# FFN passages reordered, tile shapes of the first mixer grouped, last square added ahead of the first filter combination

## The reference

```python
for i in range(DEPTH):                      # DEPTH = 2, both token groups
    m = adaln(c, w_mod[i], b_mod[i])        # shift, scale, gate, twice
    h = modulate(x, m[0], m[1])             # rms_norm(x) * (1 + scale) + shift
    x = x + m[2] * mixer_i(h)               # 0: GLA || GQA, 1: Hyena || MLA
    x = x + m[5] * swiglu(modulate(x, m[3], m[4]), w_ffn_in[i], w_ffn_out[i])
y = rms_norm(x) * g_final
```

## Time and profile before

| | us |
|---|---|
| median of 3 runs | 1628.18 (1627.47 to 1628.45) |
| the profiled execution | 1625.22 |
| its span, first to last instruction | 1622.6 |
| PE busy | 1581.8 |
| DVE busy | 1080.9 |
| ACT busy | 736.9 |

### The profile page before, as it was taken

How to read it: one execution, slowest core, us unless ns; L and a number is a source line. 1 busy time by engine, 2 the same in 40 slices (tenths; PEclk the granted TensorE clock), 3 DMA queues, 4 the chain that set the end, 5 groups by cost and what they waited for, 6 DMA issues and landing times.

```text
span 1622.6 us, 27752 instructions
## 1 busy us (share of the span) xinstructions
PE 1581.8 (97%) x11361; PEld 1462.3 (90%) x11361; DVE 1080.9 (67%) x1874; ACT 736.9 (45%) x1308; POOL 35.5 (2%) x41
## 2 busy tenths in 40 slices
PE   6999999999999999999999999999999999999997
PEld 3588897799989999999999996789999999999997
DVE  5634662768857857856874466855888487587486
ACT  5445363646624524423545434344565154254254
POOL 0000000001000000000002002000100000000000
PEclk9999999999999999999999999999999999999999
DMA  9565422035455544545235112002523223232222
GB/s 320 191 219 193 156 80 95 24 94 120 118 148 158 152 119 139 149 137 156 72 95 165 55 43 87 26 1 74 114 79 95 62 79 104 60 97 82 76 66 91
DMA packets 239335, 178.20 MB, mean 110 GB/s; under 512 B 9429, under 2 KB 232843, under 8 KB 238572
## 3 DMA queue, kind: packets, MB, share of 16 engines
q1 hardware_dynamic: 236276, 171.19, 35.0%
q0 software_dynamic: 2016, 4.59, 2.1%
q10 hardware_dynamic: 920, 0.69, 0.2%
HBM read 163.37 MB, written 8.49 MB: 106 GB/s over the span
## 4 chain that ended last, share of the span: by engine, by line
PE 90%; DVE 3%; ACT 3%; SPq 2%; DMA 1%; issue 1%; ACTq 0%; DVEq 0%
PE ua L1123 7%; PE ub L1123 7%; PE ua L1125 7%; PE ua L1124 7%; PE ub L1125 6%; PE ub L1124 6%; PE ua L1587 6%; PE ua L1589 5%; PE ua L1588 5%; PE ub L1587 5%; PE ub L1589 5%; PE ub L1588 5%; PE pm L1037 2%; PE ua L1432 2%; PE pt L1459 1%; SPq L722 1%
## 5 line engine op out<-in xcount | busy, mean ns | idle before, releaser
L2183 ACT ACTIVATE whi<-weight_sums 128x1024 fp32r<-128x1024 f32 x88 | 93.1, 1058 | 71.7 <-DVE weight_sums L2878 47.1
L1587 PE MATMUL ua<-x_mixed_high,whi 128*128 128x322 f32 x352 | 110.6, 314 | 1.9 <-ACT snap L2257 1.8
L1587 PE MATMUL ub<-x_mixed_high,whi 128*128 128x322 f32 x352 | 111.0, 315 | 0.9 <-ACT snap L2257 0.9
L1589 PE MATMUL ua<-x_mixed_high,wlo 128*128 128x322 f32 x352 | 109.2, 310 | 0.0
L1589 PE MATMUL ub<-x_mixed_high,wlo 128*128 128x322 f32 x352 | 109.2, 310 | 0.0
L1588 PE MATMUL ub<-x_mixed_rest,whi 128*128 128x322 f32 x352 | 109.0, 310 | 0.0
L1588 PE MATMUL ua<-x_mixed_rest,whi 128*128 128x322 f32 x352 | 109.0, 310 | 0.0
L2851 DVE TENSOR_TENSOR wlo<-weight_sums,whi 128x1024 fp32r<-128x1024 f32 x88 | 107.2, 1218 | 1.5 <-ACT whi L2183 1.4
L1123 PE MATMUL ub<-hidden_high,whi 128*128 128x384 f32 (+1 forms) x324 | 101.7, 314 | 4.5 <-DVE x L2946 3.5
L1123 PE MATMUL ua<-hidden_high,whi 128*128 128x384 f32 (+1 forms) x324 | 101.0, 312 | 1.6 <-DVE x L2946 1.6
L1125 PE MATMUL ub<-hidden_high,wlo 128*128 128x384 f32 (+1 forms) x324 | 100.1, 309 | 0.0
(11 more groups left out here) (688 smaller groups left out, 4959.8 us busy)
## 6 DMA issues: line engine op xcount, KB each, us to landing
raw<-in_w_ffn_in SPq DMA_DIRECT2D x88, 512.0 KB, 6.0
mod_late<-in_w_mod SPq DMA_DIRECT2D x24, 1024.0 KB, 5.3
raw<-in_w_ffn_out SPq DMA_DIRECT2D x48, 384.0 KB, 4.4
modw<-in_w_mod SPq DMA_DIRECT2D x17, 1024.0 KB, 5.4
raw<-in_w_in_even SPq DMA_DIRECT2D x10, 1024.0 KB, 7.8
raw<-in_w_in_odd SPq DMA_DIRECT2D x7, 1024.0 KB, 5.6
mod_first<-in_w_mod SPq DMA_DIRECT2D x5, 1024.0 KB, 12.3
ssq<-sq POOLq DMA_DIRECT2D x14, 320.0 KB, 4.7
```

Of the source, the lines that this page charges most:

```text
L1587: pe.matmul(dst, wh[:, c], xh, start=first, stop=False, skip_group_check=True)
L1589: ins = pe.matmul(dst, wl[:, c], xh, start=False, stop=last, skip_group_check=True)
L2183: act.activation(ring(whi, g, w), src, ACT.Copy).then_inc(g_hi, 1)
```

## The change

Six edits. SP loads the second of the two late w_mod blocks of an output pass behind the loads for m = 7 instead of m = 5. In the first mixer the w_mod blocks 10 and 11 go ahead of unit 3, and blocks 12 to 23 go to slots of the units, most of them to a slot that has a level pass, ahead of it. GLA's output runs a chunk's four full-array products first, then its eight with 64 rows; the first product into a bank alone opens it. In an output pass with six steps tile 1 is first run up to two steps before the end; tile 0 is completed, then tile 1's last two steps follow. In the beginning ACT rounds the first weights behind the decays 3 and 4, and DVE adds the last square ahead of combination 0. `hidden_last` makes the hidden product ahead of `out_rest(e, 2)`, and in every group the hidden rest ahead of `out_rest(e, 3)`.

```diff
+        MOD_SLOTS = {4: {7: (12, 13)}, 5: {3: (14,), 10: (15,)}, 6: {3: (16,), 10: (17,)}, 7: {2: (18,), 10: (19,)},
+                     8: {2: (20,), 10: (21,)}, 9: {2: (22,), 10: (23,)}}
...
-                        if (e, m) in LATE_OUT:
-                            late_mod_load(LATE_OUT[e, m])
+                        if m in (2, KD - 1) and (e, min(m, 5)) in LATE_OUT:
+                            late_mod_load(LATE_OUT[e, min(m, 5)])
...
+            def mods_at(a, n):
+                for m in MOD_SLOTS.get(n, {}).get(a, ()):
+                    mod_mm(m, mod_buffer(m))
+
+            def level_with_mods(a, p, n):
+                mods_at(a, n)
+                level_pass(p, n)
...
-                at = {a: (lambda p=p: level_pass(p, n)) for a, p in LEVEL_SLOTS.get(n, {}).items()}
+                at = {a: (lambda a=a, p=p: level_with_mods(a, p, n)) for a, p in LEVEL_SLOTS.get(n, {}).items()}
+                at |= {a: (lambda a=a: mods_at(a, n)) for a in MOD_SLOTS.get(n, {}) if a not in at}
...
-                if mods:
-                    mod_mm(mods[0], mod_buffer(mods[0]))
-                    if n == MOD_AT:
-                        mod_mm(mods[1], mod_buffer(mods[1]))
+                if n not in MOD_SLOTS:
+                    for m in mods_in(n):
+                        mod_mm(m, mod_buffer(m))
...
-                     turned=n in (VA_U, VA_U + 1, VG_U), middle=middle if inside else None,
-                     slots=head_slots(n))
+                     turned=n in (VA_U, VA_U + 1, VG_U), slots=head_slots(n))
...
                 for g in range(HP):
-                    parts = [(va[:, c, (2 * g + a) * DV:(2 * g + a + 1) * DV], sct[:, c, 2 * g + a, :], a)
-                             for a in range(2)]
...
+                    for a in range(2):
+                        ins = pe.matmul(banks[OUT_BANKS[c][a]][:, g * P:(g + 1) * P],
+                                        va[:, c, (2 * g + a) * DV:(2 * g + a + 1) * DV], sct[:, c, 2 * g + a, :],
+                                        start=g == 0, stop=c == TT - 1, skip_group_check=True)
+                if c < TT - 1:
+                    for g in range(HP):
+                        for d in range(2):
+                            for a in range(2):
...
                 kt = GROUP[e]
+                ahead = (kt - 1, kt - 2 if kt == max(GROUP) else kt - 1)
                 for m in range(2):
                     fast_out_begin(e, m)
-                    fast_out_part(e, m, 0, kt - 1)
+                    fast_out_part(e, m, 0, ahead[m])
                 for m in range(2):
-                    fast_out_part(e, m, kt - 1, kt).then_inc(p_dn, 1)
+                    fast_out_part(e, m, ahead[m], kt).then_inc(p_dn, 1)
...
             filter_decay(2)
             norm_scale(0)
-            w_high(0, 0, KD * EVEN_COLS[0][1])
             for t in range(3, TT):
                 filter_decay(t)
+            w_high(0, 0, KD * EVEN_COLS[0][1])
...
+            add_square(0, KD - 1)
             filter_combine(0)
-            add_square(0, KD - 1)
             filter_combine(1)
...
                 up_second(f)
+                hidden_product(f)
                 out_rest(e, 2)
-                hidden_product(f)
-                if e % NG < NG - 1:
-                    out_rest(e, 3)
                 hidden_rest(e, f)
-                if e % NG == NG - 1:
-                    out_rest(e, 3)
+                out_rest(e, 3)
```

More of the change, by code:

```diff
@@ L1345, in _ @@
             for n, (c0, w) in enumerate(EVEN_COLS):
-                mods = mods_in(n)
-                inside = mods if n > MOD_AT else ()
-                def middle():
-                    mod_mm(mods[1], mod_buffer(mods[1]))
                 if n < 2:
@@ L1394, in _ @@
                 for g in range(HP):
-                    parts = [(va[:, c, (2 * g + a) * DV:(2 * g + a + 1) * DV], sct[:, c, 2 * g + a, :], a)
-                             for a in range(2)]
[L1397 to L1403, removed]
+                    for a in range(2):
[6 more added lines that the diff above has]
+                            for a in range(2):
+                                rows = slice(64 * a, 64 * a + 64)
+                                ins = pe.matmul(banks[OUT_BANKS[c][a]][:, g * P:(g + 1) * P], st[rows, d, c, g],
+                                                blocks_qk[rows, (QF, QB)[d], g, c * P:(c + 1) * P],
+                                                start=False, stop=d == 1, skip_group_check=True)
                 ins.then_inc(o_mm, 1)
```

## The result

The changed kernel takes 1611.9 us (median of 4 runs, 1609.1 to 1613.5), the kernel before beside it 1627.8: a ratio of 0.9905, with a 95% interval from 0.9892 to 0.9918. The forecast was 1613.5. The profiled execution took 1611.8, with a span of 1609.5, 13.1 less than the span of before.

The account below looks back on a forecast made before the run. PE, working 1581.8 of 1622.6 us, was taken to bound the kernel. Terms 3.3 + 2.1 + 1.6 + 4.5 + 1.3 + 1.9 = 14.7 came off a median of 1628.2, giving 1613.5, range 1611 to 1621.5.

Parts of the forecast that it names:

- blocks 2.1: w_mod blocks joined with each other or with level passes: twelve fewer changes of tile shape at 0.175 us, 2.1 gained.
- GLA 1.6: GLA's output: longer runs between changes of tile shape save 0.40 us in each of four chunks, 1.6.
- six banks 4.5: Output passes e = 1 to 6: tile 2's waits for tile 0's bank go, with the slow products behind them, 4.5 us.
- hidden rest 1.3: Pass e = 0: PE's 1.02 us wait for the hidden rest goes, 1.3 gained with the slow product.
- late load 1.9: Pass e = 0: weights of m = 6 and 7 load sooner, PE's 1.60 us idle ahead of tile 5 goes, 1.9 gained.
- Both go behind: Pass e = 0: two weight rests, 0.68 and 0.69 us, leave the hidden rest's path on DVE, 1.37 or more.
- The beginning: First mixer's start: combination 3 comes 3.3 us earlier on DVE, so 3.3 is gained; bounds 1.6 to 3.7.
- the earlier sum of squares gives the root nothing, and nobody waits for it: Beginning: ACT's decay 2 waits for combination 0 ahead of the norm's root, so adding the last square first gains nothing there.
- 1.7 for the half clock: Beginning: 3.5 us at half clock behind PE's wait for a filter combination go, half of it, 1.7, being lost time.
- (b): FFN output passes: waits move to tile 3 or a weight rest, 4.5 + 1.3 + 1.9 lost, 1621.2 us; chance 0.08.
- (c): Joined blocks and level passes: the clock falls behind narrow tiles, 1627 to 1641 us; chance 0.04 slower, 0.03 about even.
- (d): Units and pass 0: w_mod blocks land late, PE waits for them, about 12 us of gain goes, 1626; chance 0.05.

Follow-up runs that it names:

- e10: Changed kernel with each w_mod block that shares a slot with a level pass put one slot earlier, apart from the pass: 1615.2 us (one run).
- e7: Changed kernel with `hidden_last` on DVE as before, two weight rests ahead of the last hidden rest: 1613.8 us.
- e8: Changed kernel with the load of an output pass's second late w_mod block back behind the load for m = 5: 1614.0 us.
- e4: Changed kernel with tile 1 of each output pass again run up to the last step but one in every group: 1616.5 us.
- e5: The changed kernel as it is, run again beside other variants: 1612.4 us.
- e11: Changed kernel with GLA's output back in the old loop over head pairs, with its flags: 1614.2 us (one run).
- e2: Changed kernel with PE's projection of filter tile 4 put ahead of the two products on modrow: 1610.1 us.
- e6: Changed kernel with filter tile 4's projection ahead of modrow's products, and tile 1 split by two steps in pass e = 0 too: 1609.6 us, 0.9887 of before.
- e9: Changed kernel with modrow's copy on DVE ahead of combination 2, and tile 1 split by two steps in pass e = 0 too: 1608.9 us, 0.9890 of before.
- e12: The kernel before, unchanged, run for a second trace: 1624.5 us.
- e1: Changed kernel with the last square again added behind combination 0 on DVE, the decays staying ahead of the first weights' rounding: 1614.2 us.

## Why the prediction was right, and where it wasn't

**Five of the six terms** were right in mechanism and size: blocks 2.1 (by difference 3.71 - 1.57 = 2.14; e10 undid eight of the twelve changes, 1.41), GLA 1.6 (1.57), six banks 4.5 (4.39), hidden rest 1.3 (1.30), late load 1.9 (1.88). What carried them is that they were taken from start to start on PE, with the slow product behind a gap, and not from idle time. The unit price of 0.175 for a change of shape held where no row had shown it, between a block and a level pass (0.176 in e10). By the Trainium skill (TensorEngine Tiling (Array Packing), Key Properties) a change of mode drains the engine while a change of tile doesn't; e10 agrees that 128 by 32 and 64 by 64 count as two modes. In the term of the hidden rest one reading was wrong. "Both go behind" holds for the second weight rest only: the first still comes ahead of the hidden rest, but behind the hidden product, where DVE has to wait for ACT's rounding anyway (0.21 is left of that wait, at 452.83). The wait of 1.02 went all the same. One small miss: "`hidden_last` of the last group in each layer changes only by the first line: 0" is 0.4 at the result's first turn (e7). It is gained in the changed kernel too, whose lead over the kernel before grows there from 12.58 to 12.95. So of the 7.78 in the table the three FFN terms gave 7.4, for 7.7 forecast. The three FFN edits undone one at a time cost 8.3; most of the 0.5 more is the 0.30 of e8's pass 1, where the kernel before lost nothing.

**The beginning** was the term that failed: 3.3 forecast, 1.46 measured in the profiled pair, of which 0.21 is an earlier start (e4, e5, e10 and e11 gained 0.5 to 0.8). DVE did as forecast: the last rest of h begins at 67.85 instead of 71.24, 3.4 earlier. The step that failed is "the earlier sum of squares gives the root nothing, and nobody waits for it". PE had waited 1.53 for it (PE's timeline, kernel before and changed kernel):

```profile
36.82 0.88 PE L1054 MATMUL ub<-ssq,ones 128*128 128x384 f32 x2 [1.53 <-DVE ssq L2478]
```
```profile
35.01 0.91 PE L1057 MATMUL ub<-ssq,ones 128*128 128x384 f32 x2
```

With the squares first, PE runs through its early products sooner and meets modrow, which combinations 0 to 2 hold back on DVE until 43.11. The wait moved there and the half clock came with it, where the prediction had it go. Of the bounds, the lower one (1.6, "if the half clock comes all the same") was the case that occurred, though behind another wait than the one it was meant for. Without the wait for modrow (e2, e6, e9) none of the three traces has a half clock, and 12 of the 13 runs have a mean clock of 0.999, which one of the changed kernel's nine has. So the wait is what let the half clock in; that it doesn't always follow, e8 shows.

The step that gave 1.7 for the half clock was wrong by itself too: e12 without it gained 0.31, since DVE's rests of h hold the first unit at nearly the same time. Where neither side has a stretch at half clock, e12 against e8, the gate unit comes at 80.32 and 76.30. 0.42 of that is an earlier start of the work ahead of it (PE's w_mod block ahead of the squares, 34.13 and 33.71); the other 3.6 is the gain of the two edits, close to the 3.3 that DVE's queue had given.

**The median.** The forecast took the profiled execution's gain and carried its distance to the median, 3.0, along. The gain in the trace was 13.4 (1625.2 to 1611.8), 1.3 less than 14.7, but the changed kernel's median lies only 0.04 above its profiled execution. So the forecast of the gain was 1.3 too high and that of the distance 2.9 too high. The two errors pull the median opposite ways, which leaves it 1.6 below the forecast; that it came so close is partly luck. Where the 3.0 sat in the kernel before is not shown: its 14 executions with a mean clock of 0.996 have a median of 1627.3, its 3 with 0.998 one of 1625.2 and its 2 with 0.999 one of 1624.7. That points to the beginning, since a trace here showed the clock below 1 only between 30 and 60 us. But no trace of a long execution was caught.

**The rivals.** Of (b) nothing came: no wait moved to tile 3 or a weight rest. Nor (c): the clock stood at 1.00 from unit 4 to 9, behind the joined blocks too. Nor (d): the blocks were there in their slots.

## What to carry to other kernels

An edit that makes one input earlier has to be followed on every engine that waits for it, also where that engine's next wait is for another thing: the time saved goes to the next wait, and on TensorE an idle stretch there may be paid twice through the clock. Fill such a stretch with work that is ready (here one exchange of two steps, 1.8 to 2.8 us by the medians). And price what a change of tile shape or a bank wait costs from start to start, the first product behind it included.

## What the runs showed of the hardware

The same idle stretch doesn't always bring the clock down. 1.20 us at 42.4 with the same work before it was followed by 7 us at 1.2 GHz in one execution and by none in another (e8). In the five other traces of that beginning 1.47 to 1.84 us were followed by 7 us four times and by 3.4 once. 2.00 and 1.75 in e12 were followed by none, 2.77 in e1 by some 10. No trace here tells what decides between them. With no idle stretch in that place (e2, e6, e9) no run had a mean clock under 0.998.
